# Slots of a weight ring that begin 16 bytes apart

## The reference, cut to what matters

```
x = x + token_mix(rms_norm(x, g), w_in) @ w_out             # layer 1: four groups of heads
x = x + (silu(conv(h @ w_up)[gate]) * conv(h @ w_up)[up]) @ w_down
x = x + rms_norm((gb * conv(gc * u)) @ w_sc_out)            # layer 2: gb, gc, u = split(h @ w_sc_in)
x = x + rms_norm(conv_ffn(h, w_up, conv, w_down))
x = x + rms_norm(sigmoid(h @ w_gate) * (p @ w_proj))
x = x + rms_norm(diff_attention(h, k, v) @ w_o)             # layer 3, then the same two lines again
```

## Time and profile before

| | |
|---|---|
| median of 3 runs | 1051.85 us (1051.77 to 1052.09) |
| span of the profiled execution | 1050.0 us |
| PE busy | 1031.0 us, 98% of the span |
| LDWEIGHTS busy (beside PE) | 959.9 us |
| DVE busy | 842.6 us, 80% |
| ACT busy | 627.5 us, 60% |
| matmuls | 8321 |

### The profile page before, as it was taken

The page is one execution under the profiler, slowest core; times in us unless marked ns, Lnnn a source line. Parts: engine busy times, 40 slices in busy tenths (PEclk is TensorE's granted clock), DMA queues, the critical chain, the costliest instruction groups (busy, mean ns, idle before and its releaser), DMA issues.

```text
span 1050.0 us, 20779 instructions
## 1 busy us (share of the span) xinstructions
PE 1031.0 (98%) x8321; PEld 959.9 (91%) x8321; DVE 842.6 (80%) x1192; ACT 627.5 (60%) x858; POOL 5.8 (1%) x16
## 2 busy tenths in 40 slices
PE   7999999999999999999999999999999999999996
PEld 6999899998999998899999999989999998999995
DVE  6966786699988878867998888779675799988876
ACT  6664556476655654546665555677576566555556
POOL 0000000000000000000000000000000000000000
PEclk9999999999999999999999999999999999999999
DMA  8432223355655544564566555344434355655531
GB/s 329 162 122 82 81 83 121 138 198 180 221 177 187 195 160 162 184 219 159 174 207 215 175 200 179 143 161 160 162 122 141 126 196 189 212 185 180 195 121 41
DMA packets 26290, 174.35 MB, mean 166 GB/s; under 512 B 3133, under 2 KB 3413, under 8 KB 6000
## 3 DMA queue, kind: packets, MB, share of 16 engines
q1 hardware_dynamic: 25520, 171.17, 47.0%
q0 software_dynamic: 704, 2.23, 0.6%
HBM read 172.33 MB, written 1.06 MB: 165 GB/s over the span
## 4 chain that ended last, share of the span: by engine, by line
PE 91%; DVE 4%; ACT 3%; DMA 1%; issue 1%; SPq 0%; DVEq 0%; ACTq 0%
PE PS L526 76%; PE PS L477 14%; ACT w_hi L1410 1%; DVE w_lo L2137 1%; DMA raw<-weights 1%; DVE h_both L2150 1%; DVE x L2682 0%; PE PS L1320 0%; DVE arena L2678 0%; ACT h_both L1427 0%; ACT xn L1482 0%; DVE arena L2676 0%; PE PS L734 0%; PE PS L704 0%; SPq L405 0%
## 5 line engine op out<-in xcount | busy, mean ns | idle before, releaser
L526 PE MATMUL PS<-h_both,w_hi 128*128 128x512 f32 (+1 forms) x1808 | 486.2, 344 | 8.7 <-DVE w_lo L2181 7.3
L2137 DVE TENSOR_TENSOR w_lo<-raw,w_hi 128x2048 fp32r<-128x2048 f32 x156 | 357.1, 2290 | 63.1 <-ACT w_hi L1410 58.3
L526 PE MATMUL PS<-h_both,w_lo 128*128 128x256 f32 (+1 forms) x1384 | 373.6, 282 | 0.0
L526 PEld LDWEIGHTS PS<-h_both,w_hi 128*128 128x128 f32 x1808 | 307.2, 189 | 53.5 <-DVE w_lo L2181 7.3
L1410 ACT ACTIVATE w_hi<-raw 128x2048 fp32r<-128x2048 f32 x157 | 299.5, 1909 | 87.7 <-PE PS L526 72.9
L526 PEld LDWEIGHTS PS<-h_both,w_lo 128*128 128x128 f32 (+1 forms) x1384 | 257.4, 190 | 0.3
L526 PE MATMUL PS<-act_hi,w_hi 128*128 128x256 f32 x704 | 198.0, 283 | 0.0
L526 PE MATMUL PS<-act_hi,w_lo 128*128 128x256 f32 x704 | 197.8, 282 | 0.0
L526 PE MATMUL PS<-act_lo,w_hi 128*128 128x256 f32 x704 | 194.9, 282 | 0.0
L526 PEld LDWEIGHTS PS<-act_hi,w_hi 128*128 128x128 f32 x704 | 133.2, 189 | 2.4 <-issue 1.4
L526 PEld LDWEIGHTS PS<-act_hi,w_lo 128*128 128x128 f32 x704 | 132.3, 188 | 0.2 <-issue 0.2
(11 more groups left out here) (337 smaller groups left out, 1119.3 us busy)
## 6 DMA issues: line engine op xcount, KB each, us to landing
raw<-weights SPq DMA_DIRECT2D x157, 1024.0 KB, 4.9
arena<-masks_in SPq DMA_DIRECT2D x1, 1472.0 KB, 12.5
x<-x_in SPq DMA_DIRECT2D x4, 256.0 KB, 4.2
raw<-weights SPq DMA_DIRECT2D x4, 256.0 KB, 5.3
raw<-weights SPq DMA_DIRECT2D x2, 512.0 KB, 9.3
arena<-bias_by_distance POOLq DMA_DIRECT2D x1, 1024.0 KB, 7.9
result<-arena SPq DMA_DIRECT2D x4, 256.0 KB, 2.0
arena<-p_in POOLq DMA_DIRECT2D x2, 256.0 KB, 4.8
```

The costliest lines, as they stand in the source:

```text
L526: return pe.matmul(o, lhs, rhs, start=start, stop=stop, skip_group_check=True)
L2137: tt(w_lo[:, slot, :], raw[:, slot, :], w_hi[:, slot, :].bitcast(F), ALU.subtract).then_inc(lo_ready, 1)
```

## The change

The slots of `w_hi` and `w_lo` are laid 2052 instead of 2048 elements apart, inside a store of 6160 elements. Slot 0 begins 0 bytes, slot 1 16 bytes and slot 2 32 bytes past a multiple of 64. Each slot is still 2048 elements without a gap inside. Each of the two stores is 64 bytes longer than before; so `w_lo` begins at byte 65728 and everything behind it 128 bytes later, all still the same distance past a multiple of 64. `raw` stays where it was. All instructions, their order, their waits and their sizes are the same on every engine; only addresses differ.

```diff
+SLOT_GAP = 4
@@
         raw = sb("raw", [P, RING, BLK])
-        w_hi = sb("w_hi", [P, RING, BLK], R)
-        w_lo = sb("w_lo", [P, RING, BLK], R)
+        def spaced(name):
+            store = sb(name, [P, RING * BLK + 16], R)
+            return store[:, 0:RING * (BLK + SLOT_GAP)].rearrange("p (s n) -> p s n", s=RING)[:, :, 0:BLK]
+
+        w_hi = spaced("w_hi")
+        w_lo = spaced("w_lo")
```

## The result

| | before | after |
|---|---|---|
| median | 1051.81 us (1050.86 to 1052.09, 4 runs) | 1045.89 us (1045.51 to 1046.03, 4 runs) |
| span of the profiled execution | 1050.0 us | 1044.0 us |
| PE busy | 1031.0 us | 1025.1 us |

A forecast was written before the change was run, and what follows sets the result against it. PE's time per matmul was taken to bound the kernel. All parts cost 0, so the span stayed 1050.0 us; with 1.85 for the median and 0.05 for the first pieces, the forecast was 1051.9, range 1049.5 to 1056.5.

The forecast's parts named there:

- the part on DMA: DMA writes `raw`, which does not move; other targets move by 128 bytes and stay the same against 64; cost 0.
- Stationary pieces: Weights PE reads as stationary operand, about 3890 matmuls in slots 1 and 2: cost 0, bounds -11.7 to +26 us.
- Lost collisions: Sign that the offset takes collisions away: row blocks under 5.6 us in slots 1 and 2 alone; chance 0.12.
- my sign of being wrong: The forecast is wrong if a row block's matmul spacing, a wide pair's or another listed distance depends on the slot.
- The argument against the collisions: Block 0's second piece, fp32r, already has an offset and keeps 117 to 118 ns a matmul.
- the small form of that rival: Collisions gone from PE's matmuls, only the 3 ns between 120 and 117: about -13 us, 1039; all collision forms 0.12.
- The rule of the Trainium skill: Matmul spacing of N / 2.4 + 2.5 ns, 109 for 256 columns; if the offset brought it back, about 1004.
- The collision: PE's operand reads against ACT's and DVE's writes to the next slots; removed by the offset, 1006 to 1040; chance 0.12.
- The slower gait: Wide blocks at 353.3 ns a pair, 6.7 more; if most go so, about 1055 to 1056.5; chance 0.05.
- the faster gait for all: None of the 60 wide blocks in the slower gait: -1.8 us, 1050.1; chance 0.03.
- Moved weights: Weights as moving operand, 496 matmuls in slots 1 and 2: cost 0, upper +3.3 us; slower rival 1055.2, chance 0.07.
- DVE, ACT, waits: Splits at worst 2364 ns, adding 7.6 us to DVE, nothing on ACT, all under PE's cover; cost 0 to +0.1 us.

The follow-up runs named there:

- the maps: PE alone, repeated series of fp32r matmuls, with only the places of stationary and moving operands shifted: 25 cases, then 47; least mean 113.3 ns a matmul.
- the first map: PE alone, 25 cases of shifted operands, each series twice: row 119.9 ns unshifted, 113.4 with both stationary 64 bytes on; wide pairs 346.8 and 353.3.
- the two best kernels: Against the kernel before: `w_lo` and everything behind it 64 bytes further, 1040.08 us; `w_hi` 64 bytes further and `w_lo` and the rest 128, 1038.73 us.
- the row series: PE alone, 48 matmuls of 256 columns in a series, the second series measured: 119.9 ns a matmul with nothing shifted.

## Why the prediction was wrong

*The failed step* is one sentence of the part on DMA: "The other targets move by 128 bytes and stay as they were against 64. Cost: 0." It was said of DMA, and `w_lo`'s 64 bytes were passed over as well. I had made "past a multiple of 64" the only measure of a place, ahead of any row that showed it, and by it I let only "those that touch a slot that now begins 16 or 32 bytes past a multiple of 64" change. The runs: these moves without any gap give 4.8 of the 5.6 us gained on that chip, 64 bytes change a matmul of 256 columns by up to 6.5 ns, and 128 bytes by 1 to 2.

*Stationary pieces, cost taken 0 [bounds -11.7 to +26 us].* The sign was that of the lower bound: 38 row blocks lost 3.6 us, 2 ns a matmul. But I had tied it to slots 1 and 2 ("Lost collisions show as row blocks under 5.6 us in slots 1 and 2 alone"), and it came in all three, at 5.66, since it isn't the slots' offset that does it here. For the same reason my sign of being wrong, a distance that depends on the slot, did not show either.

*The argument against the collisions* rested on block 0, where a piece 48 bytes off was followed at 117 ns and aligned ones at 120, and I wrote "an offset costs nothing there" and that block 0 "keeps 117 to 118". The 3 ns tempt one to see in them the effect itself, since in the maps shifted pieces take 117.8 to 118.4 and aligned ones 120.0. The trace of before doesn't bear that out. Block 0's first piece begins at a multiple of 64, and the same three distances on it are as short:

```profile
11.14 0.28 PE L526 MATMUL PS<-h_both,w_lo 128*28 128x256 f32 x1
...
11.50 0.28 PE L526 MATMUL PS<-h_both,w_lo 128*128 128x256 f32 x1
```

In whole nanoseconds these starts are 353 apart, and the shifted piece's, 12.21 and 12.56, are 351. So these rows told nothing of an offset, for or against. I priced 3 ns, in the small form of that rival, at -13 us and 1039, and asked only whether an offset could cost.

The rule of the Trainium skill that I set beside it ("TensorE: Matmul & The Clock Gate", "Back-to-back issue gap", 109 ns) was reached in no layout; the least mean of any series was 113.3 ns. The page gives it for a matmul by itself, and says that in a stream of weight loads and matmuls both set the spacing, which I left out. The rule has no place for the operands, and the runs say that the spacing depends on it.

*The collision was looked for in the wrong pair.* I named PE's reads against the writes of ACT and DVE. The effect is there with PE alone, and goes by the places of PE's own two operands. The sentence on the ports being apart thus told nothing against it.

*The slower gait.* Priced at 6.7 ns a pair, which was right, and its faster form ("the faster gait for all", given 0.03) came true beside the rest. By their pairs 16 blocks went so before (the seventeenth was at the usual gait with a stall in it), and none after; the ten blocks over 5.60 us that are left have stalls of 70 ns and more in them. Those stalls are why the wide blocks gained 0.7 us in all and not 1.7. "Identical instructions with identical durations give identical phases" failed at its condition.

*Moved weights.* Costed 0 with +3.3 as the upper end. Two of the last five blocks went from 5.44 us each [PE starts 1017.64 and 1023.08] to 5.55 and 5.59 [1011.29 and 1016.84]: 4.6 and 6 ns for a matmul of 512 columns, near the rival's price. But the first of the two is in slot 0, and without the gaps both take 5.55 in either trace: the places again, and 0.04 us for the gap of slot 1. With PE alone the price was met for matmuls of 512 moving columns, 5.0 and 6.7 ns for 16 and 32 bytes, but the rival's mechanism isn't shown by it: 64 bytes, which add no piece of 64, cost 2.2 ns too, and matmuls of 256 columns get faster by the same shifts.

*DVE, ACT, waits:* right. The split takes 2293 ns in place of 2292, against the 2364 that I had as its worst, and an offset of 16 or 32 bytes costs those two engines nothing that shows: the greatest times of the split and the rounding are 2294 and 1926 ns, against 2295 and 1924.

*An error in the part on the kernel:* it says that `act_hi` begins at a multiple of 64. By the kernel's own sizes it begins at byte 212448, which is 32 past one, and 96 past a multiple of 128. `w_hi`, `w_lo` and `h_both` all began at multiples of 128. So row blocks and wide blocks started from different distances. That is part of why they answered to the same move in different ways, but not all of it: in the first map they do so from the same places. A table of bases modulo 256 would have shown that all four distances, from `w_hi` and `w_lo` to `h_both` and `act_hi`, were about to change, by 128 and by 64 bytes.

*What stays open:* why a distance of 64 bytes is good in one order of work and not in another, what decides which of its gaits a layout falls into, and whether that lies in SBUF or in PE's own sequence. In the nine wide blocks of the two best kernels three stalls changed the gait and one didn't, and what tells them apart the traces don't say. The runs show the effect with PE alone and a repeat every 256 bytes of one operand; they don't show its mechanism.

## What to carry to other kernels

Where PE is the bound and its fp32r matmuls start over 113 ns apart at 256 columns, write down the byte at which each stationary and each moving operand begins, modulo 256, and try other distances between them: here a padding of 64 bytes, twice, and no other edit gave 1.2%. Look for the layout with a kernel that has PE alone and the true order of blocks, since series of a single kind misled here, and expect a layout to have more than one pace: trace more than one run. And when an edit adds padding, cost the move of all that is allocated behind it; a comparison without the padding's effect needs a twin that has the same bases.

## What the runs showed of the hardware

- With PE alone, successive fp32r matmuls of 256 columns on 128 x 128 pieces start 113.3 to 120.0 ns apart, at a granted clock of 0.998 or more, by the relative place of their operands in SBUF; a pair of 512 and 256 columns takes 340 to 354 ns. The extra over 106.6 ns of columns that the prediction took as fixed (13.4 ns) isn't fixed.
- A shift of 4 bytes already takes the row series from 119.9 to 118.3 ns.
- The same code at the same places runs steadily at 113.3 or 117.8 ns at two points of one program.
- 16 or 32 bytes more on moving fp32r weights: a matmul of 512 columns goes from 226.7 to 231.7 and 233.3 ns, one of 256 from 120.0 to 118.7 and 116.7.
- An offset of 16 or 32 bytes from a multiple of 64 has no cost in DVE's subtraction or in ACT's rounding of 128 x 2048 (2293 and 1910 ns, against 2292 and 1909).
